# A fused mixer block on one Trainium2 core: GpSimd's masks and scalings of the delta rule's inverses given to VectorE, and the convolution's mean square taken token by token

## What is computed

```python
decay = jnp.exp(jnp.where(tril, gc[..., :, None] - gc[..., None, :], -jnp.inf))
lmat = jnp.where(strict, jnp.einsum('nbhid,nbhjd->nbhij', kb, kc) * decay, 0.0)
tmat = triangular_solve(eye + lmat, eye, left_side=True, lower=True)
u = jnp.einsum('nbhij,nbhjd->nbhid', tmat, vb)
w = jnp.einsum('nbhij,nbhjd->nbhid', tmat, kb * jnp.exp(gc)[..., None])
```

```python
y = conv(a, conv_w) + conv_b
return jax.nn.silu(rmsnorm(y, g_conv))      # y * rsqrt(mean(y*y, axis=-1) + EPS) * g_conv
```

## Time and profile before

| | |
|---|---|
| median of three runs | 3161.66 us |
| the profiled execution | 3162.44 us |
| its span | 3159.4 us |
| TensorE busy | 3079.5 us (97%) |
| VectorE busy | 1744.8 us (55%) |
| ScalarE busy | 1169.8 us (37%) |
| GpSimd busy | 68.1 us (2%), 73 instructions |
| TensorE's granted clock | 0.994 of full speed |

### The profile page before, as it was taken

How to read it: one execution, slowest core, us unless ns; L and a number is a source line. 1 busy time by engine, 2 the same in 40 slices (tenths; PEclk the granted TensorE clock), 3 DMA queues, 4 the chain that set the end, 5 groups by cost and what they waited for, 6 DMA issues and landing times.

```text
span 3159.4 us, 42758 instructions
## 1 busy us (share of the span) xinstructions
PE 3079.5 (97%) x17790; PEld 2474.6 (78%) x17790; DVE 1744.8 (55%) x2350; ACT 1169.8 (37%) x1696; POOL 68.1 (2%) x73
## 2 busy tenths in 40 slices
PE   7999999999999999999999999999999999999998
PEld 5777856788888888877788888788888767888886
DVE  5477564534354344688764344743446877643446
ACT  4433243423243223356442223432233474422233
POOL 0012300000000000000000000000000000000000
PEclk9999999999999999999999999999999999999999
DMA  6110045333223323321232332333222212233232
GB/s 263 34 33 29 18 146 180 108 100 99 95 94 100 97 97 89 97 82 54 94 100 94 100 97 90 121 99 97 97 87 95 87 54 94 94 100 100 94 93 87
DMA packets 83615, 299.27 MB, mean 95 GB/s; under 512 B 9824, under 2 KB 11232, under 8 KB 81504
## 3 DMA queue, kind: packets, MB, share of 16 engines
q1 hardware_dynamic: 83424, 296.55, 28.9%
HBM read 290.23 MB, written 6.29 MB: 94 GB/s over the span
## 4 chain that ended last, share of the span: by engine, by line
PE 90%; DVE 4%; issue 2%; ACT 2%; DMA 0%; SPq 0%; DVEq 0%; ACTq 0%
PE PS L1931 79%; PE PS L2031 3%; PE PS L2281 1%; PE PS L1947 1%; PE PS L2265 1%; PE PS L2236 1%; ACT SPL L2336 1%; DVE SM L2974 1%; PE PS L2224 1%; PE PS L2160 1%; PE PS L2255 0%; PE PS L2290 0%; PE PS L2301 0%; PE PS L2216 0%; DVE CA L3064 0%
## 5 line engine op out<-in xcount | busy, mean ns | idle before, releaser
L1931 PE MATMUL PS<-HS,SPL 128*128 128x512 f32 x7752 | 1800.6, 392 | 8.1 <-DVE HS L2711 3.5
L1931 PEld LDWEIGHTS PS<-HS,SPL 128*128 128x128 f32 x7752 | 1449.6, 188 | 333.5 <-issue 23.9
L2656 DVE TENSOR_TENSOR SPL<-RAW,SPL 128x1024 fp32r<-128x1024 f32 (+1 forms) x483 | 580.4, 1205 | 730.0 <-ACT SPL L2336 726.0
L2336 ACT ACTIVATE SPL<-RAW 128x1024 fp32r<-128x1024 f32 (+1 forms) x483 | 499.4, 1038 | 846.2 <-PE PS L1931 845.8
L1931 PE MATMUL PS<-FF,SPL 128*128 128x512 f32 x2880 | 654.6, 389 | 0.0
L1931 PEld LDWEIGHTS PS<-FF,SPL 128*128 128x128 f32 x2880 | 540.6, 188 | 112.2
L3064 DVE SCALAR_TENSOR_TENSOR CA<-AP__151,CW,CA 128x512 f32<-128x512 f32 x240 | 179.5, 748 | 6.2
L2546 ACT ACTIVATE FF<-TMP 128x512 fp32r<-128x512 f32 x88 | 55.7, 633 | 236.4 <-DVE TMP L3034 236.4
L2540 ACT ACTIVATE SA<-SA 128x512 f32<-128x512 f32 x88 | 55.5, 633 | 191.7 <-DVE SA L3024 191.7
L3024 DVE TENSOR_TENSOR SA<-PS,R 128x512 f32<-128x512 f32 x88 | 60.5, 692 | 98.8 <-PE PS L1931 98.5
L3036 DVE TENSOR_TENSOR FF<-TMP,FF 128x512 fp32r<-128x512 f32 x88 | 60.9, 693 | 66.3 <-ACT FF L2546 66.3
(11 more groups left out here) (307 smaller groups left out, 2206.0 us busy)
## 6 DMA issues: line engine op xcount, KB each, us to landing
RAW<-in_w_ff_in SPq DMA_DIRECT2D x176, 512.0 KB, 3.7
RAW<-in_w_in SPq DMA_DIRECT2D x88, 512.0 KB, 3.7
RAW<-in_w_ff_out SPq DMA_DIRECT2D x80, 512.0 KB, 3.6
RAW<-in_w_ff SPq DMA_DIRECT2D x64, 512.0 KB, 3.7
MW<-in_w_mod SPq DMA_DIRECT2D x32, 512.0 KB, 4.4
RAW<-in_w_out SPq DMA_DIRECT2D x24, 512.0 KB, 3.8
MW<-in_w_mod SPq DMA_DIRECT2D x8, 1024.0 KB, 19.1
RAW<-in_w_ple_gate SPq DMA_DIRECT2D x16, 512.0 KB, 4.0
```

Source lines behind the costliest of these rows:

```text
L1931: m = pe.matmul(o, w[x][:, r.kp + k, rows], r.T[:, r.k0 + k, y, 0:r.cols], start=r.start and k == 0 and (x, y) == (0, 0), stop=r.stop and ...
L2336: a.activation(SPL[:, s, 0, 0:n], RAW[:, s, 0:n], AF.Copy).then_inc(w_hi, 1)
L2656: v.tensor_tensor(SPL[:, s, 1, 0:n], RAW[:, s, 0:n], SPL[:, s, 0, 0:n], ALU.subtract).then_inc(w_lo, 1)
```

## The change

All masks but the first of level 1 (into E, now L3243) go from GpSimd to VectorE: the mask into T, made right ahead of the subtraction in `inv_y`, and the masks into E of `inv_a`. The three scalings of `inv_scale` go to VectorE too. In PLAN `inv_a` is now emitted for VectorE ahead of ScalarE, and the entries of WORK are changed to suit, so `weave` makes another list for all engines. The convolution's mean square is made by token, its sums due after 6 blocks and its spreading after 7, and `conv_output` waits until the spreading is in the list.

```diff
-        "inv_a": (("PE", 0.95), ("ACT", 0.6), ("POOL", 1.2)), "inv_b": (("PE", 1.9), ("DVE", 1.37)), "inv_scale": (("POOL", 3.4),),
+        "inv_a": (("PE", 0.95), ("ACT", 0.6), ("DVE", 0.69)), "inv_b": (("PE", 1.9), ("DVE", 1.37)), "inv_scale": (("DVE", 2.1),),
...
-        J.t, J.y = count(ig[a]), count(iv[a])
+        J.t, J.y = count(iv[a]), count(iv[a])
...
-            emit("inv_a", s, "POOL", True)
+            emit("inv_a", s, "DVE")
             emit("inv_a", s, "ACT")
...
-        m_cv = stats_end(mst, RCV[:, :], ACC[:, :], width=512, after=2)
+        cv = stats_by_token(mst, RCV[:, :], ACC[:, :], (6, 7), width=512)
         cp_ready = [None] * 4
 
         def conv_output():
+            while not cv.done:
+                yield 1
             for j in range(4):
                 q = Rec()
-                q.j, q.rms, q.waits = j, m_cv, [as_ready[3]]
+                q.j, q.rms, q.waits = j, cv.done, [as_ready[3]]
...
         def inv_y(J):
             E_, LT, T_, P_ = SETS[J.a]
+            v.wait_ge(landed["msk"], 16)
+            v.wait_ge(*J.kept)
+            v.tensor_tensor(T_[:, :, :], LT[:, :, :], bc_mat(MSK[:, J.dd, 0, :]), ALU.mult).then_inc(iv[J.a], 1)
             v.wait_ge(*J.t)
             v.tensor_tensor(y_of(J), bc_mat(idc[:, :]), T_[:, :, :], ALU.subtract).then_inc(iv[J.a], 1)
+
+        def inv_a(s):
+            if not s.next:
+                return
+            E_, LT, T_, P_ = SETS[s.J.a]
+            v.wait_ge(*s.u1.mark)
+            v.tensor_tensor(E_[:, :, :], LT[:, :, :], bc_mat(MSK[:, s.J.dd, s.lv + 1, :]), ALU.mult).then_inc(ig[s.J.a], 1)
+
+        def inv_scale(J):
...
+            v.tensor_tensor(chunked(T_[:, :, :]), tokens(VST), by_chunk(beta), ALU.mult).then_inc(ig[J.a], 1)
+            v.tensor_tensor(chunked(LT[:, :, :]), tokens(KTK), by_chunk(bneg), ALU.mult).then_inc(ig[J.a], 1)
+            v.tensor_tensor(KE[:, J.dd, 4 * J.q:4 * J.q + 4, :, :], tokens(KTK), by_chunk(ed), ALU.mult).then_inc(ig[J.a], 1)
```

More of the change, by code:

```diff
@@ L2867, in inv_y, with by_chunk, chunked, tokens @@
             E_, LT, T_, P_ = SETS[J.a]
+            v.wait_ge(landed["msk"], 16)
+            v.wait_ge(*J.kept)
+            v.tensor_tensor(T_[:, :, :], LT[:, :, :], bc_mat(MSK[:, J.dd, 0, :]), ALU.mult).then_inc(iv[J.a], 1)
             v.wait_ge(*J.t)
             v.tensor_tensor(y_of(J), bc_mat(idc[:, :]), T_[:, :, :], ALU.subtract).then_inc(iv[J.a], 1)
+        def inv_a(s):
[5 more added lines that the diff above has]
+        def inv_scale(J):
+            E_, LT, T_, P_ = SETS[J.a]
+            def by_chunk(cols):
+                x = cols[:, 24 * J.dd:24 * J.dd + 24].rearrange("p (a c) -> p c a", a=2)[:, 4 * J.q:4 * J.q + 4, :]
+                return x.unsqueeze(3).to_broadcast([128, 4, 2, 64])
+            def chunked(t):
+                return t.rearrange("p (c a) n -> p c a n", a=2)
+            def tokens(t):
+                return t[:, :, 4 * J.q:4 * J.q + 4, :].rearrange("p a c n -> p c a n")
+            for w in (G.beta, G.bneg, bd["v", 0], bd["v", 1], bd["t", 0], bd["t", 1], J.last.mark, *J.ke_home):
+                v.wait_ge(*w)
+            v.tensor_tensor(chunked(T_[:, :, :]), tokens(VST), by_chunk(beta), ALU.mult).then_inc(ig[J.a], 1)
+            v.tensor_tensor(chunked(LT[:, :, :]), tokens(KTK), by_chunk(bneg), ALU.mult).then_inc(ig[J.a], 1)
+            v.tensor_tensor(KE[:, J.dd, 4 * J.q:4 * J.q + 4, :, :], tokens(KTK), by_chunk(ed), ALU.mult).then_inc(ig[J.a], 1)
         def inv_b(s):
@@ L3180, in _ @@
                 "head_recip": head_recip, "head_scale": head_scale, "head_rope": head_rope, "head_add": head_add,
-                "inv_g": inv_g, "inv_exp": inv_exp, "inv_l": inv_l, "inv_y": inv_y, "inv_b": inv_b, "oo_zero": oo_zero,
+                "inv_g": inv_g, "inv_exp": inv_exp, "inv_l": inv_l, "inv_y": inv_y, "inv_a": inv_a, "inv_scale": inv_scale, "inv_b": inv_b, "oo_zero": oo_zero,
                 "scan_0": scan_0, "scan_a": scan_a, "scan_c": scan_c, "delta_ms": delta_ms,
@@ L3211, in inv_l @@
             g.wait_ge(*J.kept)
-            g.tensor_tensor(T_[:, :, :], LT[:, :, :], bc_mat(MSK[:, J.dd, 0, :]), ALU.mult).then_inc(ig[J.a], 1)
             g.tensor_tensor(E_[:, :, :], LT[:, :, :], bc_mat(MSK[:, J.dd, 1, :]), ALU.mult).then_inc(ig[J.a], 1)
[L3215 to L3239, removed]
         def conv_pad(L):
@@ L3249, in conv_pad @@
                 g.wait_ge(*set_[1])
-        does = {"c_column": c_zero, "zeros": zeros, "inv_l": inv_l, "inv_a": inv_a,
-                "inv_scale": inv_scale, "conv_pad": conv_pad}
+        does = {"c_column": c_zero, "zeros": zeros, "inv_l": inv_l,
+                "conv_pad": conv_pad}
         for kind, r, on in STEPS:
```

## The result

The changed kernel takes 3170.78 us (median of 10 runs, 3166.64 to 3174.21), the one before 3162.52 (10 runs, 3159.81 to 3166.17). The ratio is 1.0023, with a 95% interval of 1.0016 to 1.0031: 7.3 us slower (5.1 to 9.8). The forecast was 3162.7. The time lies inside the range of 3152 to 3174, but above the line of 3168.0 from which the prediction calls the kernel slower.

The account below looks back on a forecast made before the run. The prediction took TensorE as the bound (90% of the chain). From the profiled 3162.44 us, - 2.9 for the convolution + 3.9 for VectorE's load gave 3163.4, or 3162.7 as a median; 8-in-10 range 3152 to 3174.

Parts of the forecast that it names:

- Part 1: Convolution's mean squares, both layers: 3.77 us removed less 2.31 added, 1.46 won per layer, 2.9 for both.
- the spreading waits: Rival at the convolution's mean square: the spreading waits as long as the product did, gain 0, 3165.6 us; chance 0.11.
- The mask's price: Inverses: a moved mask takes 0.61 to 0.69 us on VectorE; the bfloat16 operand was the unknown.
- The relief: VectorE's operations that GpSimd's masks disturbed, 200 to 440 us: 3.9 us of VectorE's time won back.
- VectorE's load: First three inverses, 200 to 280 us: VectorE at 84% makes TensorE idle 3.9 us more.
- for 280 to 400 I add nothing: Stretch 280 to 400 us: VectorE only comes to 75%, so nothing is added to TensorE's 4.4 us idle.
- The list itself is another one ... has no price by a row: All engines' instruction order: the new list was priced at nothing, since the sum of TensorE's work is the same.
- The granted clock is 1.00 in all of them, and I expect no change of it: Stretches from 200 to 500 us: the clock stays at 1.00, 2.4 GHz.
- w_out's start: Output product behind the attention: its start moves 2 to 10 us later; more than 10, or earlier, means wrong.
- VectorE becomes the bound: Rival among the inverses: masks waiting for products hold VectorE's queue, half of 25.4 us lost, 3171.5 us; chance 0.24.
- The forecast's own case: Whole kernel: a time within -3 to +5 us of 3162.7; chance 0.48.
- Masks sooner: Rival among the inverses: masks come sooner, their chain shortens, half of 12.4 us idle goes, 3152.6 us; chance 0.17.

Follow-up runs that it names:

- e1_conv: Kernel before with only the convolution's mean square made by token, masks and scalings still on GpSimd; 3157.26 us, ratio 0.9984.
- e5_masks_only: Kernel before, its order kept, with the convolution's mean square by token and the 30 masks on VectorE, scalings on GpSimd; 3157.42 us, ratio 0.9985.
- e3_engines: Kernel before, with its WORK, order and convolution kept, but masks and scalings executed by VectorE; 3167.58 us, ratio 1.0018.
- e4_list: Kernel before with the changed WORK and order, GpSimd still executing masks and scalings, convolution as before; 3170.65 us, ratio 1.0029.
- e9_spread: Kernel before, its order kept, plus convolution part, masks and scalings on VectorE, each scaling issued behind a following VectorE step; 3159.91 us, ratio 0.9987.
- e7_list_masks: Kernel before with only the masks' WORK entry and place changed, GpSimd executing all masks and scalings; 3164.27 us, ratio 1.0013.

## Where the prediction was right and where it failed

*Part 1* was right in mechanism and in its sum. The wait of 2.67 us went in both layers, no new one came, and the spreading's cover of 12 matmuls held. Forecast 1.46 us per layer, read 1.6. That the two agree so well is in part luck, for the terms were taken from durations, and products overlap. From start to start the product with ones cost 0.53 us and not 1.10 (1518.09 to 1518.62), the sums 0.81 and not 1.02, the spreading 0.80 and not 1.05. So 3.20 were removed and not 3.77, and 1.61 added and not 2.31. (The 1.04 us for the sums in the chain of 4.4 should be 1.02; nothing hangs on it.) The whole measured -5.1 (-7.9 to -2.2) holds the forecast 2.9; the trace of `e1_conv` has one more wait less, 0.94 us at 2415.70. The rival "the spreading waits" fell.

*The mask's price* was right: 0.68 us for one, 0.61 from start to start in a row, no effect of the bfloat16 operand.

*The relief* came, but no gain from it was measured. The forecast 3.9 us are 2.2 at the softmax rows (11.5 to 9.3) and 1.6 at the rotation (4.4 to 2.8). The disturbance of the softmax rows came from GpSimd's scalings and not from its masks: the row of 1.38 us at 283.30 starts inside the scaling of 283.21 to 284.26. By the rule that I weighed (the Trainium skill, page "SBUF — State Buffer", section "Who interferes with whom") the remaining six masks of GpSimd would hold up the new mask into T or the subtraction. The trace did not put that to the test. In all six inverses GpSimd's mask has ended before VectorE's mask into T starts (207.60 against 208.07 at the closest), and the masks into T take 0.681 us. Where two masks do meet, the trace agrees with the rule: 1.35 us in place of 0.68, 0.89 in the other case, so 0.9 us in all against a relief of 3.9. `e5_masks_only`, with the masks and the rotation's relief, has the time of `e1_conv`, so neither is on the path. The softmax rows' relief comes only with the scalings, and no run has it apart from their cost.

*VectorE's load* is the first step that failed. Its sum (+3.9) came near the +5.7 of `e3_engines` by luck. I took TensorE's loss from how full VectorE is in 20 us, and put all of it at 200 to 280, where 15 masks fall. There VectorE's load came as forecast (68.6 us of 80 in `e3_engines`, forecast 67.6; 66.5 in the changed kernel, whose list has less there), but `e3_engines` has only 0.45 us more idle time of TensorE (0.80 to 1.25). From 280 to 400 it has 4.6 more (4.36 to 8.96). The masks left no idle time at 19.05 of 20 us. What costs is the nine scalings at 279 to 284, which I had counted as load of a stretch at 75% with room to spare. They stand in front of a softmax row that TensorE wants at once: the step "for 280 to 400 I add nothing". An average over a stretch could not show it; the list, read at the place where the scalings fall, might have.

*"The list itself is another one ... has no price by a row"* is the step that cost the most. I set it to nothing because the sum of TensorE's work is the same. Its price is +9.2 us (5.7 to 12.3) in `e4_list`. The five changed orders show that it has little to do with what the new entries say: among the six that of before is the best, and every new one leaves other waits.

*"The granted clock is 1.00 in all of them, and I expect no change of it"* failed too. It is 0.97 and 0.95 in two of the three stretches. What it cost can be read, from one execution of each, against `e1_conv`, whose TensorE does the same products in another order: in the changed kernel's span of 3168.4 us TensorE is busy 3086.1 and idle 82.3, in that of `e1_conv` (3153.7) busy 3079.6 and idle 74.1. So of 14.7 us 8.2 are idle time and 6.5 the same work done more slowly.

*w_out's start* was to move by 2 to 10 us, or the forecast would be wrong, and it moved by 22.0. So by the prediction's own sign the forecast was wrong. Against `e1_conv`, where these products start at 499.94, the move is 22.7 and the spans differ by 14.7, so some 8 us of the move are work done earlier (modulation columns, and four of the eight products with the embedding that stood at the next mean square), and the rest is loss.

*The rivals.* "VectorE becomes the bound" gave 3171.5, close to the measured 3170.78, but its reason holds at most for the 5.7 of the some 15 us that the two causes lost. The forecast's own case ended at 3167.7; the time is in the range only because the range takes in half of this rival. The time lies there mostly through a cause, the order, that stands in none of the terms, and that is luck. "Masks sooner" won nothing: `e5_masks_only` has the idle time of before, so the chains of the inverses were not what TensorE waited for.

The best kernel is not the changed one. `e1_conv` (3157.26) beats both, and `e5_masks_only` (3157.42) can't be told from it.

## What to carry to other kernels

Where a planner's table sets the order of every engine, a change of a number in it is a change of the whole kernel: give it its own run, with the old order kept by hand, before anything is said of the edit itself. And price a moved operation at the place where it lands, by what stands behind it in that engine's queue and who waits for it; here nine scalings of 5.4 us in a row, in front of a softmax row that the bounding engine wanted, cost a wait of 5.2 us, and thirty masks elsewhere, where that engine had other products, nothing that was measured. To spread the nine among the same softmax rows did not take the idle time away.

## What the runs showed of the hardware

Idle time of TensorE can have a second price. Behind a wait of 5.20 us (`e3_engines`) the same products took 5.41 us in place of 3.39, at the lower of the two clock levels (1.2 in place of 2.4 GHz). Behind two waits of 2.32 and 0.98 us, with products from 311.93 to 312.56 between them, the product with KH took 0.79 in place of 0.50. About the same idle time in seven pieces of at most 1.54 us (`e9_spread`, 4.89 us of the slice from 280 to 300) left the clock at 1.00. The clock also fell where no wait was longer than 1.37 us (0.83 from 400 to 420 in `e5_masks_only`), so these runs give no rule. In four of the five kernels of which only the list was changed the lower mean clock makes 4.4 to 5.2 us by the estimate above, beside 4.2 to 9.2 of idle time; in `e7_list_masks` 0.5 beside 1.3.

In the changed kernel a mask of VectorE took 1.35 us in place of 0.68 beside a mask of GpSimd (327.83), and a mask of GpSimd 1.54 in place of 1.16 (206.06) beside VectorE's scaling of AQ, which reads AQ and SR from SBUF.
